# Experts' gate and up products of a two-layer decoder: the weights become the stationary operand, the tokens move, and an expert has 96 places for tokens instead of 128

## What is computed

```python
D_MODEL, N_EXPERTS, TOP_K, D_FF_EXPERT = 1024, 8, 2, 3584

def moe_swiglu(h, w_router, w_gate, w_up, w_down):
    logits = (ht @ w_router)                       # 256 x 8
    top_vals, top_idx = lax.top_k(logits, TOP_K)
    gates = jax.nn.softmax(top_vals, axis=-1)
    ...                                            # xs: each token twice, sorted by expert
    g = lax.ragged_dot(xs, w_gate, group_sizes)    # 1024 -> 3584, weights of the token's expert
    u = lax.ragged_dot(xs, w_up, group_sizes)
    y = lax.ragged_dot(jax.nn.silu(g) * u, w_down, group_sizes)   # 3584 -> 1024
    ...                                            # times the gate, summed per token
```

## Time and profile before

| what | value |
|---|---|
| median of 3 runs | 1617.76 us (1612.77 to 1621.94) |
| the profiled execution, its own time | 1623.15 us |
| its span in the trace | 1621.4 us |
| TensorE matmul busy | 1529.0 us, 94% of the span |
| weight loads busy | 1227.4 us, 76% |
| VectorE busy | 1156.3 us, 71% |
| ScalarE busy | 955.5 us, 59% |
| mean granted clock of TensorE | 0.954 of full |

### The profile page before, as it was taken

How to read it: one execution, slowest core, us unless ns; L and a number is a source line. 1 busy time by engine, 2 the same in 40 slices (tenths; PEclk the granted TensorE clock), 3 DMA queues, 4 the chain that set the end, 5 groups by cost and what they waited for, 6 DMA issues and landing times.

```text
span 1621.4 us, 20186 instructions
## 1 busy us (share of the span) xinstructions
PE 1529.0 (94%) x7621; PEld 1227.4 (76%) x7621; DVE 1156.3 (71%) x1199; ACT 955.5 (59%) x924; POOL 66.8 (4%) x89
## 2 busy tenths in 40 slices
PE   6985979999889879999999999999999999999996
PEld 3775669999646467887887887887887887887884
DVE  6663225545236178888888888888988888888885
ACT  4243135444235257776776777777777777777773
POOL 2640000000010000000000000000000000000000
PEclk9997989999985979999999999999999999999997
DMA  7324934527420229999999999998998998998990
GB/s 229 112 39 51 366 107 178 182 104 253 162 104 1 104 103 329 370 346 333 370 340 338 370 337 337 368 356 317 370 370 307 369 375 306 365 372 315 359 366 27
DMA packets 197456, 425.94 MB, mean 263 GB/s; under 512 B 18850, under 2 KB 27904, under 8 KB 197376
## 3 DMA queue, kind: packets, MB, share of 16 engines
q1 hardware_dynamic: 197104, 425.23, 73.8%
q10 hardware_dynamic: 304, 0.06, 0.0%
HBM read 421.67 MB, written 1.05 MB: 261 GB/s over the span
## 4 chain that ended last, share of the span: by engine, by line
PE 84%; DVE 6%; ACT 5%; issue 3%; DMA 1%; POOL 0%; ACTq 0%; DVEq 0%
PE bank L633 63%; PE bank L385 4%; PE bank L600 3%; PE bank L362 3%; PE bank L431 3%; PE bank L738 2%; ACT w_hi L1271 2%; PE bank L749 2%; DVE w_lo L1638 1%; PE bank L585 1%; PE bank L515 1%; PE bank L563 1%; ACT L1296 1%; DVE work L1485 1%; DMA ring<-in_l_w_in 1%
## 5 line engine op out<-in xcount | busy, mean ns | idle before, releaser
L1638 DVE TENSOR_TENSOR w_lo<-ring,w_hi 128x2048 fp32r<-128x2048 f32 x342 | 780.6, 2291 | 126.1 <-ACT w_hi L1271 123.3
L1271 ACT ACTIVATE w_hi<-ring 128x2048 fp32r<-128x2048 f32 x342 | 652.7, 1917 | 143.6 <-PE bank L633 141.7
L633 PE MATMUL bank<-w_hi,xg_hl 128*128 128x512 f32 x1792 | 565.3, 397 | 2.7 <-DVE xg_hl L1692 2.7
L633 PEld LDWEIGHTS bank<-w_hi,xg_hl 128*128 128x128 f32 x1792 | 333.6, 188 | 77.7 <-issue 10.6
L633 PE MATMUL bank<-w_lo,xg_hl 128*128 128x512 f32 x896 | 350.4, 391 | 0.0
L633 PE MATMUL bank<-w_hi,at_hl 128*128 128x512 f32 x896 | 283.2, 397 | 0.0
L633 PEld LDWEIGHTS bank<-w_hi,at_hl 128*128 128x128 f32 x896 | 167.1, 188 | 39.3 <-issue 3.8
L633 PEld LDWEIGHTS bank<-w_lo,xg_hl 128*128 128x128 f32 x896 | 168.6, 188 | 36.3
L633 PE MATMUL bank<-w_lo,at_hl 128*128 128x512 f32 x448 | 175.7, 392 | 0.0
L1565 DVE TENSOR_TENSOR fpart_hl<-ring,fpart_hl 128x1024 fp32r<-128x1024 f32 x66 | 80.7, 1226 | 94.1 <-ACT fpart_hl L1209 93.6
L633 PE MATMUL bank<-ht_hl,fpart_hl 128*128 128x256 f32 x1056 | 130.3, 286 | 3.7 <-DVE ht_hl L1576 2.1
(11 more groups left out here) (213 smaller groups left out, 1078.0 us busy)
## 6 DMA issues: line engine op xcount, KB each, us to landing
ring<-in_l_moe_w_gate SPq DMA_DIRECT2D x58, 2048.0 KB, 7.8
ring<-in_l_moe_w_up SPq DMA_DIRECT2D x57, 2048.0 KB, 7.8
ring<-in_l_moe_w_down SPq DMA_DIRECT2D x56, 2048.0 KB, 7.9
ring<-in_l_ffn_w_gate SPq DMA_DIRECT2D x5, 2048.0 KB, 8.1
ring<-in_l_ffn_w_up SPq DMA_DIRECT2D x5, 2048.0 KB, 8.0
ring<-in_l_ffn_w_down SPq DMA_DIRECT2D x5, 2048.0 KB, 7.8
ring<-in_l_w_in SPq DMA_DIRECT2D x4, 2048.0 KB, 8.6
ring<-in_l_w_out SPq DMA_DIRECT2D x4, 2048.0 KB, 9.0
```

Source lines behind the costliest of these rows:

```text
L633: last = mm(p, lhsT=xs[a], rhs=ws[b], start=start and q == 0, stop=stop and q == 2, **kw)
L1271: ac(w_hi(n), at(e_slot(q) * SLOT + j * HALF, HALF), ACT.Copy).then_inc(S("hi"), 1)
L1638: tt(LO[e_slot(q)][:, j * HALF:(j + 1) * HALF], at(e_slot(q) * SLOT + j * HALF, HALF), w_hi(n).bitcast(fp), ALU.subtract).then_inc(S("lo"), 1)
```

## The change

`CAP` goes from 128 to 96: an expert has 96 places. In the gate and up products `three` now gets the weights as `xs` (stationary, blocks of 128 rows x 128 hidden columns) and the tokens as `ws` (moving, 96 columns). The result comes out with hidden units as rows, four blocks of 96 columns in one PSUM bank, so `flip` goes, and ScalarE and VectorE fill `AT` from `HID` itself. `AT` keeps 128 columns; the last 32 are set to zero once, ahead of the experts. TensorE waits for a new semaphore `at_lo` ahead of a down item, and VectorE for the same ahead of overwriting `HID`.

```diff
-CAP = 128
+CAP = 96
 PASSES = -(-T // CAP)
...
-        PER = [4, 4, 3, 3, 1, 1, NC_E + 1, 6]
+        PER = [4, 4, 3, 3, 1, 1, 1, 6]
...
-                def flip(c):
-
-                    read_out(pe, (key, "gu", c, 1), turn)
-                    p = unit(pe, (key, "aT", c), 6, turn)
-                    for f in range(4):
-                        last = transpose(p[:, f * CAP:(f + 1) * CAP], HID[0:CAP, f * P:(f + 1) * P], CAP)
-                    ready(last, (key, "aT", c))
...
-                            read_out(pe, (key, "aT", c), turn)
+                            pe.wait_ge(S("at_lo"), turn.count("at_lo", c + 1))
...
-                                last = three(acc[b][0:CAP, :], (AT[c % 2][:, 0, f], AT[c % 2][:, 1, f]),
+                                last = three(acc[b][:, :], (AT[c % 2][:, 0, f], AT[c % 2][:, 1, f]),
                                              [w_[:, o:o + 512] for w_ in hl],
...
-                        for a in range(4):
-                            k = 4 * j + a
-                            last = three(p[0:CAP, :], (XG[:, 0, k], XG[:, 1, k]),
-                                         [w_[:, a * 512:(a + 1) * 512] for w_ in hl], k == 0, k == KT - 1)
+                        for f in range(4):
+                            for a in range(4):
+                                k, o = 4 * j + a, a * 512 + f * P
+                                last = three(p[:, f * CAP:(f + 1) * CAP], [w_[:, o:o + P] for w_ in hl],
+                                             (XG[:, 0, k], XG[:, 1, k]), k == 0 and f == 0, k == KT - 1,
+                                             skip_group_check=True)
...
-                    if n in FLIP_AT:
-                        flip(FLIP_AT[n])
...
-                        free(ac(SG1[0:CAP], p[0:CAP, :], ACT.Silu), (key, "gu", c, 0))
+                        free(ac(SG1, p[:, 0:4 * CAP], ACT.Silu), (key, "gu", c, 0))
                     if k in FLIP_AT:
-                        p = got(act, (key, "aT", FLIP_AT[k]), turn)
-                        ac(AT[FLIP_AT[k] % 2][:, 0].rearrange("p f t -> p (f t)"), p[:, 0:4 * CAP], ACT.Copy).then_inc(S("hi_small"), 1)
+                        read_out(act, (key, "gu", FLIP_AT[k], 1), turn)
+                        ac(AT[FLIP_AT[k] % 2][:, 0, :, 0:CAP], HID.rearrange("p (f t) -> p f t", f=4), ACT.Copy).then_inc(S("hi_small"), 1)
...
-                        free(tt(HID[0:CAP], SG1[0:CAP], p[0:CAP, :], ALU.mult), (key, "gu", c, 1))
+                        if c:
+                            dve.wait_ge(S("at_lo"), turn.count("at_lo", c))
+                        free(tt(HID, SG1, p[:, 0:4 * CAP], ALU.mult), (key, "gu", c, 1))
...
-                        free(tt(a_hl[:, 1].rearrange("p f t -> p (f t)"), PS[6][:, 0:4 * CAP],
-                                a_hl[:, 0].rearrange("p f t -> p (f t)").bitcast(fp), ALU.subtract), (key, "aT", FLIP_AT[k]))
+                        tt(a_hl[:, 1, :, 0:CAP], HID.rearrange("p (f t) -> p f t", f=4), a_hl[:, 0, :, 0:CAP].bitcast(fp),
+                           ALU.subtract).then_inc(S("at_lo"), 1)
```

More of the change, by code:

```diff
@@ L170, in trunk @@
         XG = hi_lo("xg_hl", C0, 2, KT, CAP)
-        AT0 = hi_lo("at0_hl", C0 + 2 * KT * CAP, 2, 4, CAP)
+        AT0 = hi_lo("at0_hl", C0 + 2 * KT * P, 2, 4, P)
         mo0 = HT0 + NH * HALF
         mo = cut(mo0, B0 + 6144)
-        PICK, PG, HID, YR, GATE, SG1 = mo(TM, CAP), mo(TM, CAP), mo(512), mo(D), mo(T), mo(512)
+        PICK, PG, HID, YR, GATE, SG1 = mo(TM, CAP), mo(TM, CAP), mo(4 * CAP), mo(D), mo(T), mo(4 * CAP)
         POS, GW = mo(TM, PASSES * NE + 1), mo(TM, PASSES * NE)
         vt = mo(14)
-        AT1 = hi_lo("at1_hl", mo0 + 2896, 2, 4, CAP)
+        AT1 = hi_lo("at1_hl", mo0 + 3072, 2, 4, P)
         LG, SEL, RNK, EX, POS0 = (mo(TM, NE) for _ in range(5))
@@ L263, in trunk @@
         TALLY = {"pick": (1, 1), "pgate": (0, 1), "hi": (0, NPT), "lo": (0, NPT),
-                 "part_used": (0, NPT - len(ends_bank)), "hi_small": (2, NC_E + 2)}
+                 "part_used": (0, NPT - len(ends_bank)), "hi_small": (2, NC_E + 2),
+                 "at_lo": (0, NC_E)}
         class Turn:
@@ L1625, in _ @@
                 got(dve, ("a1", "O", ng - 1, a))
-            v.memset(YR, 0.0)
+            link(v.memset(YR, 0.0))
+            none = YR[:, 0:4 * (P - CAP)].rearrange("p (f t) -> p f t", f=4)
+            for a_hl in AT:
+                for x in range(2):
+                    tt(a_hl[:, x, :, CAP:P], none, none, ALU.subtract)
             v.memset(GATE, 0.0)
```

## The result

The changed kernel takes 3161.95 us (median of 4 runs, 3147.24 to 3165.45) where the kernel before takes 1619.85 us: a ratio of 1.949, 95% interval 1.942 to 1.957. I had forecast 2220 us, 2125 to 2370. The direction was right, and the size was not: +1542 us instead of +598.

A forecast was written before the change was run, and what follows sets the result against it. TensorE was taken to bound each 126.2 us turn: less 77.3 for gate and up and 2.5 for the flip, plus 1344 pairs at 0.115 us (154.6), gives 201.0; eight turns add 598 us, forecasting 2220 us, range 2125 to 2370.

The forecast's parts named there:

- three rows: Trace rows bounding a gate/up load-and-matmul pair: line 715 106 ns, line 447 114 ns, gather and 256-column matmuls 112 to 121.
- The gather's row: Gather's 128 x 128 blocks with 128 columns: 32 instructions in 3.73 us, 117 ns each, or 112 in the chain.
- The way from line 447's short loads: Line 447's 63 ns pace with 32-row loads, plus 51 ns for a full block's longer load: 114 ns, taken as 115.
- The flip: Four gate transposes the change removes, priced at 0.36 us, seven times a turn: 2.5 us saved.
- The remainder of 46.4 us: Rest of a turn without gate, up and flip, claimed unchanged: 126.2 - 77.3 - 2.5 us.
- the clock falls: Rival: TensorE granted 0.50 for parts of the loop, pairs 213 ns; a tenth at half clock gives 2360 us; 9%.
- Load and matmul in a row: Rival: gate/up load and matmul don't overlap, 159 ns a pair, 2694 us; 9% together with the dearer price.
- a dearer price under 256 columns: Rival: few moving columns charged as plain float32, 168 ns a pair, 2791 us; 9% together with load and matmul not overlapping.
- Cheap load: Rival: a float32r block loads as fast as line 447's, 63 ns a pair, 1662 us, still slower; 3%.
- Faster: Rival: loads hide wholly and columns pace gate and up, 53 ns a pair, 1554 us; 2%.
- The second loop over experts: Rival: an expert with over 96 tokens starts a second loop, 16 more turns of 201 us, 5400 us; 1%.
- The edits at no cost: VectorE and ScalarE work, transfers (219 GB/s), the at_lo wait and zeroing AT's spare columns were claimed to cost nothing that counts.

The follow-up runs named there:

- e3: Kernel before, tokens still stationary and flip kept, each gate and up matmul of 512 columns split into four of 128: 2433.20 us, ratio 1.504.
- e9: Changed kernel with stationary blocks 64 hidden columns wide instead of 128, half of the hidden units left out in gate and up: 1624.58 us, ratio 1.002.
- e7: Changed kernel with 32 moving columns instead of 96 in gate and up, the other 64 places left out: 3236.71 us, ratio 1.997.
- e5: Changed kernel with 128 places instead of 96, so 128 columns move, and no zeroing of spare columns: 2346 us.
- e10: Changed kernel with each w_hi block loaded once for the tokens' high and low parts (192 columns), w_lo once for 96; four repeat runs: median 1877.46 us, ratio 1.162.
- e11: Changed kernel plus one useless matmul of 512 columns ahead of every 12 pairs of 96 columns: 2585.09 and 2627.04 us.
- e2: Kernel before (128 places, tokens stationary) without the flip's transposes, so its result is another one: 1588.48 us, ratio 0.981.

## Why the prediction was wrong, point by point

**What bounds the kernel: right.** TensorE did before and does after; for VectorE's w_lo it waits in e3 (2.1 to 2.8 us a turn) and in e9, not in the changed kernel.

**The terms of the sum: right, at full clock.** The pair was taken as 115 ns from three rows (106, 112 to 117, 121); it is 111 to 112 with 96 and 128 columns, paced by the load (e7, e9). The gather's row was the best of the three. The way from line 447's short loads came out 3 ns high. The flip was 0.52 us and not 0.36, 3.65 a turn and not 2.5. Part of that stood in the trace one row further on: the two matmuls behind the flip start at 703.99, and the next, below, at 704.54, 0.55 later where two steps are 0.46.

```profile
704.54 0.39 PE L633 MATMUL bank<-w_lo,at_hl 128*128 128x512 f32 x1
```

The remainder of 46.4 us came out at 46.7 (e5's turn of 197.2 us at full clock less 1344 x 0.112) and 47.0 (e10's of 147.4), in part by luck: with the flip at 3.65 it would have been 45.2, and the pause of 1.0 to 1.5 us a turn ahead of the first gate matmul was not in the sum.

**The step that failed: the rival "the clock falls".** I gave it 9% and priced one tenth of the loop at half clock. It came true for 80% of a turn's time. The prices were good: a turn wholly at half clock stood there as 373 us, one at full is 197, and 80% of the time at the one and 20% at the other give 1 / (0.80 / 373 + 0.20 / 197) = 316 us, against 320.8 measured. How the kernel would pay was there, with its rows; how likely and for how long was not, and the main sum had the clock's fall at nothing. It is worth about 989 of the 1542 us (under e11). I had argued that the page shows 9 "wherever TensorE had worked without a pause", and that it would go on working without one. It did: 97% busy, and the clock still halved. A busy share does not tell whether the clock stays; in the experts' loop before, no stretch had full loads with 96 or fewer columns behind them, and ahead of it the longest was line 715's 6 us or so. That row was at 0.50 in the earlier trace rows, and I read it for the load's price alone. Its own matmuls can hardly have lowered the clock, since the first of them began at 563.76 at full clock, behind a pause of 1.93 us, and the clock was down from 564.1 on:

```profile
563.76 1.50 PE L715 MATMUL bank<-work 128*128 128x8 f32 x8 [1.93 <-ACT work L1077]
...
563.70:564.10 0.40, 0.34 (x4) 1.00 1.05 410
564.10:570.10 6.00, 6.00 (x31) 0.50 0.33 123
```

But it stayed down through 6 us of such pairs without a pause. That was the one warning in the trace, and a weak one. Line 447, which I held against this rival, has loads of 32 rows.

**The other rivals.** Load and matmul in a row, or a dearer price under 256 columns: excluded, 32, 96 and 128 columns all run at 111 to 114 at full clock. Cheap load: excluded for full blocks. A rule of the Trainium skill ("TensorE: Matmul & The Clock Gate", LDWEIGHTS: columns divided by 1.2 GHz, 107 ns for 128) lies within 5 ns of the pair here at full clock; by the same rule 64 columns are 53 as an estimate, and e9 shows 60. At half clock the pair is 214, twice the rule's figure. The Trainium skill's 81 ns for a pair with 128 moving columns ("TensorE: Matmul & The Clock Gate", Back-to-back issue gap) was not reached: 112 here. Faster: excluded. The second loop over experts: did not run, the loads are 58 + 57 + 56 as in the earlier trace rows.

**The edits at no cost.** ScalarE and VectorE stayed at 91 and 109 us a turn as expected, 28% and 34% of the longer turn where 46% and 55% had stood, and TensorE never waited for `at_lo` or anything of theirs in the turn shown. The loads ran at 138 GB/s, not 220, since the turn was longer. The one pause of 1.3 us in it had been costed at nothing; what it waits for is open.

**A version that beats both kernels** was not found: e2 is faster by 30 us, but it leaves the transposing out. Its 30 us for the flip is an upper bound of what a cheaper transpose can give.

## What to carry to other kernels

Count a matmul's price as the larger of its columns and its load, and keep the operand with many columns moving: 12 matmuls of 512 columns cost 2.8 us, and 48 of 96 columns, with a quarter fewer columns in all, 5.4 at best. Then ask what the clock will do: a stream of full loads with few columns behind each may be granted 1.2 GHz although TensorE is never idle, and that costs as much again. Where a layout forces such pairs, put more columns behind each load (high and low part together gave back 1284 of 1542 us) before trimming places, and look for a pause ahead of a long stretch of them: with 128 columns the clock fell only behind one.

## What the runs showed of the hardware that was not expected

- The clock goes to half in a stream without pauses: 0.58 over 310 us in which TensorE was busy throughout. Full loads of 128 columns at 1344 a turn: with 32 columns behind each a mean of 0.64 over the span, with 96 0.65 to 0.68, with 128 0.88 to 0.90, with 256 0.97, where the last is 1.00 through the loop. With loads of 64 columns, 96 columns behind each are granted 1.00 through the loop in two decimals (0.96 over the span).
- With 128 columns behind each load the clock fell only within 2.3 us behind a pause of 1.0 to 2.8 us (12 of 14 pauses in e3 and e5), and then stayed at half for 51 to 65 us of pairs. With 256 columns seven pauses of 0.9 to 1.2 us were followed by no fall.
- More work can be faster: 256 columns instead of 96 by 905 us, and a useless matmul of 512 columns to every 12 pairs by 535 to 577.
- A pair paced by a full load takes 111 to 114 ns at full clock, and 210 to 214 at half, with 32, 96 or 128 columns behind it (128 at half: 143 pairs in 30.3 us of e5).
- Stationary blocks of 96 columns instead of 128 load in 162 ns instead of 188 and make nothing faster where 512 columns hide them; the kernel was 0.45% slower.
